# The first norm's root multiplies the products instead of the input

## The chip, the cores and the metric

One NeuronCore of a Trainium2 chip runs the kernel. The metric is device time in microseconds (us) of one execution.

## The reference

Two transformer blocks on x [256, 2048] in float32. What matters here is the first lines of the first block:

```
def _rmsnorm(x, w):
    y = x32 * lax.rsqrt(jnp.mean(x32 * x32, axis=-1, keepdims=True) + RMS_EPS)
    return (y * w.astype(jnp.float32)).astype(x.dtype)

u = _rmsnorm(h, norm_mix_w[l])                      # h = x, [256 tokens, 2048]
proj = jnp.einsum('btd,de->bte', u, w_in[l])        # w_in [2048, 11280]
(q_a, k_a, v_a, z_a, beta_a, dec_a, q_b, k_b, v_b, gate_a, gate_b) = jnp.split(proj, ...)
# q_a, k_a, v_a: causal convolution over 4 tokens, silu; then a gated delta rule with
# beta = sigmoid(beta_a), g = -exp(a_log) * softplus(dec_a + dt_bias)
# z_a: silu;  q_b, k_b, v_b: attention;  gate_a, gate_b: sigmoid
```

The root is one number for each token (row of x), so `proj = root * ((x * w) @ w_in)`: it can be multiplied before or after the product. The rest of the block (delta rule, attention, branch mix, feed-forward) and the second block stand behind this.

## The kernel before, in words

Every large product runs on TensorE in units. A unit is 256 rows of a weight matrix by 512 columns (512 KB). SyncE loads it into one of four slots of `raw` (RING = 4), ScalarE rounds it to `w_hi` (float32r), VectorE subtracts to get `w_lo`, and TensorE multiplies three times (hi by hi, lo by hi, hi by lo) against the input, which is split in the same way into `u_hi` and `u_lo`. The semaphores are `w_landed`, `hi_done`, `lo_done` and `w_used`; the load of a unit waits until the unit four before it has its `w_lo`, and the cast of a unit waits until TensorE has used the unit four before it. PLAN gives the order of the products: "qkv" (3 bodies of 16 units, 24 matmuls of 128x256 each unit, output transposed, channels on partitions), "spill" (8 bodies of 16 units, 12 matmuls of 128x512 each, tokens on partitions: z, q_b, k_b, v_b and the two gates), then "branch", "w_out", "ffn" and the products of the second block. A body makes 1024 columns, the first 512 in banks 0 and 1, the others in banks 2 and 3. Smaller work is put between the units by hand: each engine has callbacks (`first_due`, `between`) that run ahead of (ScalarE, VectorE) or behind (TensorE) unit j of a body.

The start. SyncE issues x in two halves of 128 tokens (1 MB each) with the constants `keep` (192 KB, the identity for transposes) between them, then the rows of `norm_mix_w`, four weight units, 17 small vectors, `ws_raw`, and the units from the fifth on. ScalarE squares each half of x with a sum (L1314), takes the root (L1306), casts the first unit. VectorE takes the reciprocal and multiplies x by it in pieces of 128x512 (`scaled_x`, L1939) into `xn`. TensorE transposes `xn`, four 128x128 tiles for each `turn_first(q)` (q = 0 to 7, two column blocks of x each, L709): q = 0 to 3 ahead of the first unit, q = 4, 5 behind unit 1 and q = 6, 7 behind unit 2. The transposes land in banks 4, 5, 2, 3 (FIRST_BANKS); ScalarE (`operand_high`, L1297) and VectorE (`operand_low`, L1917) multiply them by the norm weight's column and split them into `u_hi` and `u_lo`.

What uses the "qkv" and "spill" products. VectorE's `conv_pair` (L2003, L2005) reads a bank of the "qkv" product and does the four taps as 8 instructions of up to 256 elements on each partition; there are 12 such calls, q = 0 and 1 at j = 9 and 11 of a body, q = 2 and 3 at j = 1 and 3 of the next (the last two are in "spill"). `thin` makes the 16 logit columns (beta_a, dec_a) in bank 6 behind unit 10. `spill_drain` on ScalarE (L1384) reads a bank of the "spill" product with an activation and stores it. `delta_net` is a generator on each of the three engines that advances one step for each unit of "spill". Its first step on ScalarE (j = 0, ahead of the cast of that unit) is sigmoid of the beta logits (L1394) and exp of `a_log` (L1395); its first step on VectorE reads the other logits (L2045, L2047, L2051); ScalarE's next step (j = 1) is exp (L1400), ln (L1401) and the first square (L1418); TensorE's third step waits for ln and the square (L771). In the third "qkv" body and in "spill" VectorE also does a vector-matrix product for the modulation (`gemv`, L1874 to L1888), one 256 KB piece of weights for each unit, in two buffers; the load of a piece waits for the step on the piece before it (`gemv_step`).

Of the kernel before, what the change touches and what calls it, by code (L numbers as in the profile page):

```python
# [25 lines left out]
P = 128  # L26
T = 256
# [85 lines left out]
def block_kernel(nc, x, norm_mix_w, w_in, conv_w, a_log, dt_bias, gdn_o_norm_w, q_norm_w, k_norm_w,  # L113
# [5 lines left out]
    with ctx:  # L119
# [37 lines left out]
        xn = slot("xn", 7, [P, HALVES, D])  # L157
# [89 lines left out]
        def h_stage(q):  # L247
# [13 lines left out]
        E6, E5, QNS, BFC, MX, SUM, RCP, LAM, RELB, FCOL, CACT = (  # L261
            179, 180, 181, 182, 192, 256, 320, 384, 400, 416, 448)
# [83 lines left out]
        x_in = (sem("x_in0"), sem("x_in1"))  # L346
# [90 lines left out]


# [9 lines left out]
        def _(sp):  # L448
            loads = signal("vectors_in")
            for th in range(HALVES):  # L450
                sp.dma_start(xs[:, th], x[0][th * P:(th + 1) * P, :]).then_inc(x_in[th], 16)
                if th == 0:
                    sp.dma_start(keep[:], keep_const[:, 0:KEEP_W]).then_inc(signal("keep_in"), 16)
# [9 lines left out]
            dst, src = pairs[0]  # L463
            sp.dma_start(dst, src).then_inc(signal("mix_in"), 16)
            for j in range(RING):
                load(products["qkv"], 0, j, w_in[0], j, 0)
# [115 lines left out]
        def _(pe):  # L582
# [116 lines left out]
            pe.transpose(bank[SPARE][:, 3 * P:3 * P + KD], rows[0:KD, 0], ident[0:KD, 0:KD]).then_inc(signal("mix_sum"), 1)  # L699

            def turn_first(q):

                pe.wait_ge(signal("xn_ready"), HALVES * (q // 2 + 1))
# [3 lines left out]
                for f in range(2):  # L707
                    for th in range(HALVES):
                        ins = pe.transpose(b[:, f * T + th * P:f * T + (th + 1) * P],  # L709
                                           xn[:, th, (2 * q + f) * P:(2 * q + f + 1) * P], ident)  # L710
                ins.then_inc(turned, 1)

            for q in range(4):
                turn_first(q)
# [17 lines left out]
            def first_due(j):  # L732
                if j in (1, 2):
                    turn_first(2 * j + 2)
                    turn_first(2 * j + 3)
                if j == 4:
                    turn_rows()
                if j == 10:
# [505 lines left out]
        def _(act):  # L1244
# [64 lines left out]

            act.wait_ge(signal("constants_set"), 1)  # L1310
            own.link(act.activation(sm(RCP + 62), sm(E6), ACT.Sqrt, bias=sm(E6)))
            for th in range(HALVES):
                act.wait_ge(x_in[th], 16)
                own.inc(act.activation(xn[:, th], xs[:, th], ACT.Square, accum_out=sm(SS + th)))  # L1314
            own.wait()
            root(0, sm(SS, HALVES), sm(RR, HALVES), 1.0 / D, E6, "root_x")
# [58 lines left out]
            def spill_drain(pr, i, x):  # L1375
# [7 lines left out]
                for th in range(HALVES):  # L1383
                    act.activation(stage[:, x, th], acc[x][th][:], func).then_inc(drained[x], 1)  # L1384
# [7 lines left out]
            def delta_net():  # L1392
                act.wait_ge(signal("logits"), 1)
# [424 lines left out]
            for i in range(2):  # L1818
                def between(j, i=i):
# [3 lines left out]
                    if i == 0 and j == 10:  # L1823

                        act.wait_ge(signal("logits"), 2)
# [25 lines left out]
        def _(dve):  # L1851
# [84 lines left out]
            def scaled_x(c):  # L1936
                part = slice(c * COLS, (c + 1) * COLS)
                for th in range(HALVES):
                    dve.tensor_scalar(xn[:, th, part], xs[:, th, part], sm(RR + th), None, ALU.mult).then_inc(  # L1939
                        signal("xn_ready"), 1)  # L1940

# [7 lines left out]
            dve.wait_ge(signal("mix_sum"), 1)  # L1949
# [6 lines left out]
            first_low(0)  # L1956
            operand_low(0)
            first_low(1)
            operand_low(1)
            scaled_x(2)  # L1960
            operand_low(2)
            first_low(2)
            operand_low(3)
            first_low(3)
# [792 lines left out]
```

## Time and profile before

| | |
|---|---|
| median of 3 runs | 2657.59 us (2654.68 to 2659.8) |
| profiled execution | 2654.59 us, of which the span is 2652.8 us |
| TensorE matmul busy | 2586.1 us (97% of the span) |
| VectorE busy | 1796.1 us (68%) |
| ScalarE busy | 1171.8 us (44%) |
| DMA | 604.69 MB, mean 228 GB/s |

The span is from the first instruction to the last. TensorE's busy time counts pipelined matmuls and is no measure of its peak; idle time of an engine matters where TensorE waits for it. In timelines and groups, PE is TensorE, PEld its weight loads, DVE VectorE, ACT ScalarE, SPq the DMA queue of SyncE. Square brackets give the idle time ahead of an instruction and what ended it.

### The profile page before, as it was taken

What the parts mean: (1) busy time and instruction counts of PE and PEld (TensorE: products, weight loads), DVE (VectorE), ACT (ScalarE), POOL (GpSimd) and SP (SyncE); (2) the same over time, 40 slices, a digit from 0 to 9 for tenths busy, and PEclk for the clock granted to TensorE, in tenths of its full rate; (3) what the DMA queues carried; (4) which work ended last, traced back from release to release, by engine and by line L of the source; (5) the groups of instructions that cost most, each with busy time, mean ns of one, the idle gap of its engine ahead of it and who ended that gap; (6) DMA issues with size and microseconds to landing.
All of it is one profiled execution on the core that took longest, in us unless ns stands there. A gap on an engine that the chain in (4) does not pass through costs nothing.

```text
span 2652.8 us, 38762 instructions
## 1 busy us (share of the span) xinstructions
PE 2586.1 (97%) x14614; PEld 2175.5 (82%) x14614; DVE 1796.1 (68%) x2331; ACT 1171.8 (44%) x1475; POOL 0.2 (0%) x4
## 2 busy tenths in 40 slices
PE   8999999998999999999999999999999999999997
PEld 8977777777788778888887888899987778999885
DVE  6787676775567777777776666766786665545655
ACT  4454333454344544444443334333486344335642
POOL 0000000000000000000000000000000000000000
PEclk9999999999999999999999999999999999999998
DMA  7667676875768788888887777888845556665363
GB/s 209 195 234 249 218 229 208 276 254 192 250 209 269 260 270 269 275 274 271 272 275 246 251 249 254 278 273 272 252 141 182 181 167 183 182 215 165 123 224 125
DMA packets 313837, 604.69 MB, mean 228 GB/s; under 512 B 26670, under 2 KB 28724, under 8 KB 312028
## 3 DMA queue, kind: packets, MB, share of 16 engines
q1 hardware_dynamic: 301628, 571.59, 67.2%
q10 hardware_dynamic: 12064, 31.10, 3.2%
q8 instruction: 99, 1.62, 0.2%
q14 instruction: 46, 0.38, 0.0%
HBM read 591.98 MB, written 10.62 MB: 227 GB/s over the span
## 4 chain that ended last, share of the span: by engine, by line
PE 74%; DVE 2%; ACT 2%; issue 1%; DMA 1%; ACTq 0%; DVEq 0%; SPq 0%
PE bank L631 18%; PE bank L633 18%; PE bank L632 18%; PE bank L654 5%; PE bank L656 5%; PE bank L655 5%; PE bank L593 1%; PE bank L1091 1%; DVE w_lo L1858 1%; ACT w_hi L1254 0%; DMA raw<-in_w_branch_gdn 0%; PE bank L1102 0%; PE bank L1112 0%; PE bank L1088 0%; PE bank L1114 0%
## 5 line engine op out<-in xcount | busy, mean ns | idle before, releaser
L1858 DVE TENSOR_TENSOR w_lo<-raw,w_hi 128x1024 fp32r<-128x1024 f32 x820 | 1001.4, 1223 | 802.1 <-ACT w_hi L1254 801.0
L1254 ACT CAST w_hi<-raw 128x1024 fp32r<-128x1024 f32 x820 | 859.9, 1050 | 1371.7 <-PE bank L633 1028.2
L631 PE MATMUL bank<-w_hi,u_hi 128*128 128x512 f32 x1216 | 493.8, 406 | 3.1 <-DVE u_lo L1917 2.2
L632 PE MATMUL bank<-w_lo,u_hi 128*128 128x512 f32 x1216 | 483.8, 398 | 0.0
L633 PE MATMUL bank<-w_hi,u_lo 128*128 128x512 f32 x1216 | 483.2, 397 | 0.0
L1883 DVE SCALAR_TENSOR_TENSOR gemv_acc<-gemv_w,small,gemv_acc 128x512 f32<-128x512 f32 x480 | 357.8, 745 | 5.6 <-DMA gemv_w<-in_w_mod 5.2
L631 PE MATMUL bank<-w_hi,s_hi 128*128 128x512 f32 x768 | 311.1, 405 | 1.2 <-DVE w_lo L1858 1.1
L633 PE MATMUL bank<-w_hi,s_lo 128*128 128x512 f32 x768 | 304.6, 397 | 0.0
L632 PE MATMUL bank<-w_lo,s_hi 128*128 128x512 f32 x768 | 304.4, 396 | 0.0
L654 PE MATMUL bank<-s_hi,w_hi 128*128 128x256 f32 x1024 | 289.5, 283 | 0.0
L655 PE MATMUL bank<-s_lo,w_hi 128*128 128x256 f32 x1024 | 288.3, 282 | 0.0
L656 PE MATMUL bank<-s_hi,w_lo 128*128 128x256 f32 x1024 | 288.3, 282 | 0.0
L631 PEld LDWEIGHTS bank<-w_hi,u_hi 128*128 128x128 f32 x1216 | 230.3, 189 | 65.6 <-issue 8.1
L633 PEld LDWEIGHTS bank<-w_hi,u_lo 128*128 128x128 f32 x1216 | 230.3, 189 | 56.2
L632 PEld LDWEIGHTS bank<-w_lo,u_hi 128*128 128x128 f32 x1216 | 230.6, 190 | 51.5
L655 PEld LDWEIGHTS bank<-s_lo,w_hi 128*128 128x128 f32 x1024 | 193.2, 189 | 0.3
L656 PEld LDWEIGHTS bank<-s_hi,w_lo 128*128 128x128 f32 x1024 | 193.2, 189 | 0.0
L654 PEld LDWEIGHTS bank<-s_hi,w_hi 128*128 128x128 f32 x1024 | 192.0, 187 | 0.7 <-issue 0.3
L633 PEld LDWEIGHTS bank<-w_hi,s_lo 128*128 128x128 f32 x768 | 144.9, 189 | 35.3
L631 PEld LDWEIGHTS bank<-w_hi,s_hi 128*128 128x128 f32 x768 | 144.9, 189 | 34.8 <-DVE w_lo L1858 1.5
L632 PEld LDWEIGHTS bank<-w_lo,s_hi 128*128 128x128 f32 x768 | 145.2, 189 | 32.7
L631 PE MATMUL bank<-w_hi,hid_hi 128*128 128x512 f32 x352 | 140.0, 398 | 0.0
(356 smaller groups left out, 2903.5 us busy)
## 6 DMA issues: line engine op xcount, KB each, us to landing
gemv_w<-in_w_mod SPq DMA_DIRECT2D x384, 256.0 KB, 3.0
raw<-in_w_in SPq DMA_DIRECT2D x176, 512.0 KB, 4.5
raw<-in_a_w_in SPq DMA_DIRECT2D x128, 512.0 KB, 4.5
raw<-in_w_ffn_gate SPq DMA_DIRECT2D x88, 512.0 KB, 4.5
raw<-in_w_ffn_up SPq DMA_DIRECT2D x88, 512.0 KB, 4.1
raw<-in_w_ffn_down SPq DMA_DIRECT2D x88, 512.0 KB, 4.0
gemv_w<-in_kv_w_mod SPq DMA_DIRECT2D x128, 256.0 KB, 3.6
raw<-in_kv_w SPq DMA_DIRECT2D x64, 512.0 KB, 3.7
```

The source lines that it names most:

```text
L593: ins = pe.transpose(b[:, f * T + th * P:f * T + (th + 1) * P], src(f, th), ident)
L631: pe.matmul(o, xh, w_hi[:, s, t], start=(k == 0), stop=False)
L632: pe.matmul(o, xh, w_lo[:, s, t], start=False, stop=False)
L633: ins = pe.matmul(o, xl, w_hi[:, s, t], start=False, stop=(k == 2 * units - 1))
L654: pe.matmul(o, wh, hi[:, k], start=(k == 0 and f % 2 == 0), stop=False)
L655: pe.matmul(o, wh, lo[:, k], start=False, stop=False)
L656: ins = pe.matmul(o, wl, hi[:, k], start=False, stop=(k == 2 * half - 1 and f % 2 == 1))
L1091: ins = pe.matmul(b[:, P:3 * P], queries_of[p][:, a, P:T], k_t[:, a, 0:T], start=True, stop=not mask)
L1254: act.copy(w_hi[:, s], raw[:, s]).then_inc(hi_done, 1)
L1858: dve.tensor_tensor(w_lo[:, s], raw[:, s], w_hi[:, s].bitcast(F32), ALU.subtract).then_inc(lo_done, 1)
L1883: dve.scalar_tensor_tensor(out=gemv_acc[:], in0=w_k, scalar=c_k, in1=gemv_acc[:], op0=ALU.mult, op1=ALU.add).then_inc(gemv_step, 1)
```

## The change

x is loaded in three column parts (0:512, 512:1024, 1024:2048, each for all 256 tokens) instead of two token halves. The rows of `norm_mix_w`, weight units 0 and 1 and the third part of x are issued by ScalarE, the rest of the start by SyncE. TensorE transposes raw x (`xs`), so `xn` and `scaled_x` are gone: q = 0 and 1 ahead of the first unit, then two more behind each of units 0, 1 and 2. ScalarE squares x at j = 3 and 4 and takes the root at j = 5, VectorE the reciprocal at j = 6 (`RX`), TensorE spreads it over all partitions as a row at j = 7 (two matmuls of 128x128) and VectorE copies it to `rx_bc` at j = 8. The products are multiplied by it where they are read: `conv_pair` gets one 128x512 multiply ahead of its taps, `spill_drain` a per-partition scale, and the two groups of logits one multiply in place in bank 6, after which ScalarE's sigmoid may start.

```
 sync:
-            for th in range(HALVES):
-                sp.dma_start(xs[:, th], x[0][th * P:(th + 1) * P, :]).then_inc(x_in[th], 16)
-                if th == 0:
-                    sp.dma_start(keep[:], keep_const[:, 0:KEEP_W]).then_inc(signal("keep_in"), 16)
+            load_x(sp, 0)
+            sp.dma_start(keep[:], keep_const[:, 0:KEEP_W]).then_inc(signal("keep_in"), 16)
+            load_x(sp, 1)
+            load_first(sp, 2)
+            load_first(sp, 3)
...
-            dst, src = pairs[0]
-            sp.dma_start(dst, src).then_inc(signal("mix_in"), 16)
-            for j in range(RING):
-                load(products["qkv"], 0, j, w_in[0], j, 0)
 tensor:
             def turn_first(q):
-                pe.wait_ge(signal("xn_ready"), HALVES * (q // 2 + 1))
+                pe.wait_ge(x_in[min(q // 2, 2)], 16)
...
-            for q in range(4):
+            for q in range(2):
                 turn_first(q)
...
-                if j in (1, 2):
+                if j < 3:
                     turn_first(2 * j + 2)
                     turn_first(2 * j + 3)
...
+                if j == 7:
+                    pe.wait_ge(signal("rx_ready"), 1)
+                    for th in range(HALVES):
+                        ins = pe.matmul(bank[MODB][:, th * P:(th + 1) * P], sm(RX + th).broadcast_to([P, P]), ident,
+                                        start=True, stop=True)
+                    ins.then_inc(signal("first_sum"), 1)
 scalar:
+            dst, src = vector_rows()[0]
+            act.dma_start(dst, src).then_inc(signal("mix_in"), 16)
+            load_first(act, 0)
+            load_first(act, 1)
+            load_x(act, 2)
...
-            for th in range(HALVES):
-                act.wait_ge(x_in[th], 16)
-                own.inc(act.activation(xn[:, th], xs[:, th], ACT.Square, accum_out=sm(SS + th)))
-            own.wait()
-            root(0, sm(SS, HALVES), sm(RR, HALVES), 1.0 / D, E6, "root_x")
...
-            first_high(0)
             act.wait_ge(signal("cols_mix"), 1)
             for q in range(4):
                 operand_high(q)
-                if q < 3:
-                    first_high(q + 1)
+                first_high(q)
...
+                if j in (3, 4):
+                    own.inc(act.activation(x_sq[:, j - 3], xs[:, j - 3], ACT.Square, accum_out=sm(SS + j - 3)))
+                if j == 5:
+                    own.wait()
+                    root(0, sm(SS, HALVES), sm(RX, HALVES), 1.0 / D, E6, "root_x")
...
-                    act.activation(stage[:, x, th], acc[x][th][:], func).then_inc(drained[x], 1)
+                    act.activation(stage[:, x, th], acc[x][th][:], func, scale=sm(RX + th)).then_inc(drained[x], 1)
...
             def delta_net():
-                act.wait_ge(signal("logits"), 1)
+                act.wait_ge(signal("logits"), 2)
 vector:
-            dve.wait_ge(signal("root_x"), 1)
-            own.link(dve.reciprocal(sm(RR, HALVES), sm(RR, HALVES)))
-            scaled_x(0)
-            scaled_x(1)
...
+            for q in range(4):
+                operand_low(q)
+                first_low(q)
...
+                if j == 6:
+                    dve.wait_ge(signal("root_x"), 1)
+                    dve.reciprocal(sm(RX, HALVES), sm(RX, HALVES)).then_inc(signal("rx_ready"), 1)
+                if j == 8:
+                    dve.wait_ge(signal("first_sum"), 2)
+                    own.link(dve.tensor_copy(rx_bc[:], bank[MODB][:, 0:T]))
...
+                own.link(dve.tensor_tensor(over_x[:, q % 2], b[:].rearrange("p (f t) -> p f t", f=2), over_heads(rx_bc[:], 2), ALU.mult))
                 for tap in range(TAPS - 1, -1, -1):
...
-                        src = b[:, f * T:(f + 1) * T]
+                        src = over_x[:, q % 2, f]
...
                 dve.wait_ge(signal("logits"), 1)
+                dve.tensor_tensor(bank[SPARE][both, 0:T], bank[SPARE][both, 0:T], rx_bc[both], ALU.mult).then_inc(
+                    signal("logits"), 1)
+                dve.wait_ge(signal("logits"), 2)
```

The two helpers that it calls:

```
        X_PARTS = (slice(0, COLS), slice(COLS, 2 * COLS), slice(2 * COLS, D))
        def load_x(engine, n):
            part = X_PARTS[n]
            engine.dma_start(xs[:, :, part], halves(x[0])[:, :, part]).then_inc(x_in[n], 16)
        def load_first(engine, j):
            src = w_in[0][2 * P * j:2 * P * (j + 1), 0:COLS].rearrange("(t p) n -> p t n", p=P)
            engine.dma_start(raw[:, j], src).then_inc(w_landed[j], 16)
```

## Rows read from the trace of the kernel before

**Rows 1.** The page: busy time, share of the span and instructions of the engines.
```profile
PE 2586.1 (97%) x14614; PEld 2175.5 (82%) x14614; DVE 1796.1 (68%) x2331; ACT 1171.8 (44%) x1475; POOL 0.2 (0%) x4
```

**Rows 2.** Timeline of all engines, 0 to 40 us: start, length, engine, line, operation, tiles.
```profile
5.67 1.91 ACT L1314 ACTIVATE xn<-xs 128x2048 f32<-128x2048 f32 x1 [3.34 <-DMA xs<-in_x]
...
9.53 0.26 PE L699 MATMUL bank<-keep,rows 16*128 16x16 f32 x1 [9.53 <-DMA rows<-in_norm_mix_w]
...
12.69 3.67 PE L709 MATMUL bank<-keep,xn 128*128 128x128 f32 x16 [2.90 <-DVE xn L1939]
13.34 1.22 DVE L1944 TENSOR_TENSOR w_lo<-raw,w_hi 128x1024 fp32r<-128x1024 f32 x1
13.90 0.84 ACT L1297 ACTIVATE u_hi<-bank,cols 128x256 fp32r<-128x256 f32 x2 [1.45 <-PE bank L709]
...
14.63 1.04 ACT L1320 CAST w_hi<-raw 128x1024 fp32r<-128x1024 f32 x1
...
16.01 0.56 PE L654 MATMUL bank<-u_hi,w_hi 128*128 128x256 f32 x1
```

**Rows 3.** DMA from 0 to 30 us in 40 slices of 0.75 us.
```profile
GB/s 0 0 87 284 404 459 316 460 382 459 327 356 369 399 407 421 393 361 209 103 34 58 335 292 150 350 227 0 57 175 388 145 238 325 156 320 249 142 202 344
```

**Rows 4.** The tile `keep`, 0 to 20 us: its load (ns, start) and landing.
```profile
L453 SPq DMA_DIRECT2D keep<-in_keep_const x1: 420/420/420, 1.2 to 1.2; - x1
...
DMA to landing us min/median/max: 4.9/4.9/4.9
```

**Rows 5.** Timeline of TensorE and ScalarE in the first product.
```profile
16.80 0.41 PE L654 MATMUL bank<-u_hi,w_hi 128*128 128x256 f32 x1
17.01 0.37 PE L655 MATMUL bank<-u_lo,w_hi 128*128 128x256 f32 x1
...
22.37 1.04 PE L709 MATMUL bank<-keep,xn 128*128 128x128 f32 x8
...
30.12 1.05 ACT L1254 CAST w_hi<-raw 128x1024 fp32r<-128x1024 f32 x1 [0.85 <-PE bank L656]
33.00 1.05 ACT L1254 CAST w_hi<-raw 128x1024 fp32r<-128x1024 f32 x1 [1.83 <-PE bank L656]
```

**Rows 6.** Timelines of four engines around the start of the spill product.
```profile
162.19 0.34 SPq L484 DMA_DIRECT2D gemv_w<-in_w_mod  x1
...
165.05 0.75 DVE L1883 SCALAR_TENSOR_TENSOR gemv_acc<-gemv_w,small,gemv_acc 128x512 f32<-128x512 f32 x1 [1.75 <-DMA gemv_w<-in_w_mod]
...
165.26 0.38 ACT L1394 ACTIVATE gates<-bank 8x256 f32<-8x256 f32 x1
...
165.66 1.28 ACT L1395 ACT_TABLE_LOAD   x1
...
167.19 1.05 ACT L1254 CAST w_hi<-raw 128x1024 fp32r<-128x1024 f32 x1
...
169.16 0.48 DVE L2045 TENSOR_SCALAR gates<-bank,small 8x256 f32<-8x256 f32 x1
...
170.51 0.42 ACT L1400 ACTIVATE gates<-gates 8x256 f32<-8x256 f32 x1 [2.28 <-DVE gates L2051]
...
173.46 1.16 PE L771 MATMUL bank<-sq,pick 128*16 128x256 f32 x4 [2.21 <-ACT sq L1418]
```

**Rows 7.** Groups by line and form: count, busy us, mean ns of one, idle before.
```profile
L1384 ACT ACTIVATE stage<-bank 128x512 f32<-128x512 f32 x32 | 17.3, 594 | 0.1
...
L1482 ACT ACTIVATE qk_t<-bank,small 128x512 f32<-128x512 f32 x4 | 2.6, 686 | 2.4 <-PE bank L593 2.3
...
L2311 DVE TENSOR_TENSOR stage<-bank,gates 128x512 f32<-128x512 f32 x16 | 10.2, 681 | 0.0
```

**Rows 8.** Windows: busy of each engine, granted clock, DMA share, GB/s.
```profile
174.00:176.00 2.00, 2.00 (x7) 1.16 (x4) 1.97 (x5) 2.00 (x4) 0.00 (x0) 0.55 0.85 305
```

**Rows 9.** The chain that ended last, 600 to 612 us.
```profile
606.62 1.09 ACT stage L1384 x2
```

More of the change, by code:

```diff
@@ L156, in block_kernel @@
         u_lo = slot("u_lo", 5, [P, KD, T], F32R)
-        xn = slot("xn", 7, [P, HALVES, D])
+        x_sq = slot("x_sq", 7, [P, HALVES, D])
+        rx_bc = slot("rx_bc", 13, [P, T])
+        over_x = slot("over_x", 13, [P, 2, 2, T], extra=1024)
         ws_raw = slot("ws_raw", 9, [P, KD, 16])
@@ L260, in block_kernel @@
         LN_STATS, LN_MOMENTS = 336, 322
-        E6, E5, QNS, BFC, MX, SUM, RCP, LAM, RELB, FCOL, CACT = (
-            179, 180, 181, 182, 192, 256, 320, 384, 400, 416, 448)
+        E6, E5, QNS, BFC, RX, MX, SUM, RCP, LAM, RELB, FCOL, CACT = (
+            179, 180, 181, 182, 184, 192, 256, 320, 384, 400, 416, 448)
         c_act = small[:, CACT:CACT + KD]
@@ L345, in block_kernel @@
         turned, turn_hi, turn_free = sem("turned"), sem("turn_hi"), sem("turn_free")
-        x_in = (sem("x_in0"), sem("x_in1"))
+        x_in = (sem("x_in0"), sem("x_in1"), sem("x_in2"))
         gemv_landed = (sem("gemv_landed0"), sem("gemv_landed1"))
@@ L698, in _ @@
             pe.wait_ge(signal("mix_in"), 16)
-            pe.transpose(bank[SPARE][:, 3 * P:3 * P + KD], rows[0:KD, 0], ident[0:KD, 0:KD]).then_inc(signal("mix_sum"), 1)
+            pe.transpose(bank[SPARE][:, 3 * P:3 * P + KD], rows[0:KD, 0], ident[0:KD, 0:KD]).then_inc(signal("first_sum"), 1)
             def turn_first(q):
-                pe.wait_ge(signal("xn_ready"), HALVES * (q // 2 + 1))
+                pe.wait_ge(x_in[min(q // 2, 2)], 16)
                 if q >= 4:
@@ L709, in turn_first @@
                         ins = pe.transpose(b[:, f * T + th * P:f * T + (th + 1) * P],
-                                           xn[:, th, (2 * q + f) * P:(2 * q + f + 1) * P], ident)
+                                           xs[:, th, (2 * q + f) * P:(2 * q + f + 1) * P], ident)
                 ins.then_inc(turned, 1)
-            for q in range(4):
+            for q in range(2):
                 turn_first(q)
@@ L1823, in between @@
                     if i == 0 and j == 10:
-                        act.wait_ge(signal("logits"), 2)
+                        act.wait_ge(signal("logits"), 3)
                         ln_weights(0)
@@ L1934, in _ @@
             dve.memset(ws_lo[:].bitcast(F32), 0.0).then_inc(signal("ws_zero"), 1)
[L1936 to L1940, printed above, removed]
             def first_low(j):
@@ L1947, in operand_low @@
                 lo_of_turn(q, q % 4, u_lo[:, 2 * q:2 * q + 2], u_hi[:, 2 * q:2 * q + 2], MIX_W + 2 * q, FIRST_BANKS)
-            dve.wait_ge(signal("mix_sum"), 1)
+            dve.wait_ge(signal("first_sum"), 1)
             dve.tensor_copy(cols[:, 0:KD], bank[SPARE][:, 3 * P:3 * P + KD]).then_inc(signal("cols_mix"), 1)
-            dve.wait_ge(signal("root_x"), 1)
-            own.link(dve.reciprocal(sm(RR, HALVES), sm(RR, HALVES)))
-            scaled_x(0)
-            scaled_x(1)
             dve.wait_ge(signal("cols_mix"), 1)
[L1956 to L1964, printed above, removed]
-            scaled_x(3)
+            for q in range(4):
+                operand_low(q)
+                first_low(q)
             def first_due(j):
@@ L2043, in delta_net @@
                 logits = bank[SPARE][hd, 0:T]
+                both = slice(0, 32 + H1)
                 dve.wait_ge(signal("logits"), 1)
+                dve.tensor_tensor(bank[SPARE][both, 0:T], bank[SPARE][both, 0:T], rx_bc[both], ALU.mult).then_inc(
+                    signal("logits"), 1)
+                dve.wait_ge(signal("logits"), 2)
                 dve.tensor_scalar(gates8[hd, 0], logits, sm(DTB, 1, 32, 40), 0.0, ALU.add, ALU.min).then_inc(
@@ L2705, in _ @@
                 body("v3", i, value_drain, between)
-            dve.wait_ge(signal("logits"), 2)
+            dve.wait_ge(signal("logits"), 3)
             z = bank[SPARE][0:H3, 0:T]
```

## The prediction

> **What bounds the kernel now.** The page comes first. TensorE is busy for 97% of the span [rows 1], so whatever starts TensorE earlier, or makes it wait, moves the end by as much, and work on other engines costs nothing unless TensorE comes to wait for it. The change touches four places only: the start, the convolutions, the logits and the drains of "spill". For each I read the timeline of the engines and ask what TensorE waits for there.
>
> At the start TensorE does nothing before 9.53, turns x from 12.69 on and begins the first unit at 16.01 [rows 2]. From there it has no gap: ScalarE's casts, each released by the end of a unit, stand 2.88 us apart (30.12 to 33.00), which is the price of a unit, 0.12 us for each of its 24 matmuls [rows 5]. The last matmuls before 17.2 start 0.21 us apart (16.80, 17.01) [rows 5], the pace of the 1.2 GHz level; the later ones run at 2.4 GHz. From 16.01 to 30.12, where unit 3 ends, there are four units (11.5), two groups of 8 transposes of 1.04 each (2.1) and about 0.6 for the slow first matmuls: 14.2 against 14.1 read.
>
> The next gap of TensorE in the stretch that the change touches is at 171: it idles 2.2 us until 173.46, put down to ScalarE's square [rows 6]. Behind the square stands a serial chain: VectorE's gates (169.16) release ScalarE's exp (170.51), then a table load, ln and the square. It is on the path, and it is where the change adds work.
>
> **The start.** Removed from the path: the squares (1.91 each, the first started when x had landed at 5.67), root, reciprocal and scaling. What then sets the first unit is the identity in `keep`, which every transpose needs. It is issued at 1.2 and lands 4.9 us later, at 6.1 [rows 4]; until then 1.25 MB (half of x, then it) had been asked for on its queue. With slices of 0.75 us the DMA row gives 1.16 MB moved by 5.25 and 1.5 MB by 6.0 [rows 3], so landing comes some 0.6 us behind the bytes. After the change 0.52 MB of x and 0.2 MB of `keep` stand on SyncE's queue, and ScalarE's queue moves about as much in the meantime: 1.45 MB, at about 5.9, landed at 6.6. The Trainium skill, "DMA: Bandwidth & Descriptors", section "Issuing engines are not separate DMA queues", says that transfers issued by several engines interleave on the same DMA engines and that this only saves issue time; no row of before has two busy queues at the start, so nothing here tests it, and by it the split buys no bandwidth. By bounds from rows: not before 6.1, where it lands today behind more bytes of its own queue; the other end is the third rival below.
>
> From 6.6: the small transpose and the first four of x. From the first transpose of x to ScalarE's first `u_hi` is 1.2 us today (12.69 to 13.90), with 0.15 more for the small one: 7.95. Two `u_hi` pieces until the cast starts take 0.73 (13.90 to 14.63), the cast 1.04, `w_lo` 1.22 [rows 2]: 7.95 + 0.73 + 1.04 + 1.22 = 10.95, say 11.0 for the first unit. That is 5.0 earlier than 16.01.
>
> Given back: one more group of 8 transposes now stands behind the first unit, 1.04; two broadcast matmuls behind unit 7, at the transposes' 0.13 each, 0.3 with their loads. And the lower level: today it costs unit 0 about 0.6, behind 16 transposes without a pause. After the change only 8 come first and TensorE idles about 2 us before unit 0. If all 24 matmuls of unit 0 then start 0.21 apart instead of 0.12, that costs 2.2, 1.6 more than today; at the other end it costs what it does now, 0 more. I take 1.1, nearer the upper end, since the run-up is half as long and followed by an idle stretch. Gain 5.0 - 1.04 - 0.3 - 1.1 = 2.6 us; bounds: 5.5 - 1.34 = 4.2 and, with `keep` 1 us later, 4.0 - 1.34 - 1.6 = 1.1.
>
> Does anything else become late? ScalarE's `u_hi` for q = 2 waits for transposes that now come behind unit 0, about 16: with cast and `w_lo` unit 2 is ready at 19.0, and TensorE wants it at about 20.4. So it is covered, by 1.4 us. The squares at j = 3 and 4 put 2.1 us each in front of two casts; a cast is needed three units (8.6 us) later and ScalarE idles 1.8 us of each 2.88: at nothing. SyncE issues three transfers fewer before the small vectors, and the next weight load then waits for `lo_done`, as before. The reciprocal and copy on VectorE stand ahead of casts that have the same ring of slack: at nothing.
>
> **The convolutions.** Each of 12 calls gets a multiply of 128x512 from a bank, 0.68 (the group at L2311) [rows 7], and a wait for its own result, some 0.06. In bodies 1 and 2 VectorE is idle part of each unit, and a late `w_lo` has the ring before it. What remains is the third body, where gemv leaves VectorE without idle time: its last idle before 169 ends at 165.05 with a landed gemv piece [rows 6], whose load was issued at 162.19, right when VectorE had finished the step before. So that idle time does not absorb a delay; it moves with it. Two calls at j = 9 and 11: 1.5 us at most, 0 at least if the backlog clears before; I take 1.0, since the load waits on VectorE's step.
>
> **The logits.** Today the wait chain is 169.16 to 173.46, 4.30 us [rows 6]. ScalarE had done sigmoid, a table load, exp and a cast long before (165.26 to 168.2), under cover of VectorE's backlog. The change makes sigmoid wait for VectorE's multiply, which comes at 169.16 plus the delay above. So on the path now: the multiply, 0.48 (as L2045, a read of the same bank); sigmoid, the exp table and exp, 167.19 - 165.26 = 1.93; the cast, 1.05; then exp to TensorE's resumption, 173.46 - 170.51 = 2.95, and 0.04 for the semaphore. That is 6.45, plus 1.0 of delay: 7.45 against 4.30, a gap longer by 3.15 us (2.15 to 3.65). Queued behind the waiting sigmoid are the cast of unit 4 of "spill", exp, ln and the square; behind the cast is VectorE's `w_lo`. TensorE needs that unit two units after it resumes, so only the square is waited for.
>
> The table load behind sigmoid takes 1.28 and the next activation starts with it done [rows 6]. The Trainium skill, "ScalarE: Activation LUTs", section "What ACT_TABLE_LOAD costs", puts a switch at about 2.66 us with a drain behind the load; the row shows no drain. By the page the one load newly on the path would cost 1.4 us more and the sum would be 1.4 us longer.
>
> The clock: after today's gap of 2.2 us the granted clock reads 0.55 from 174 to 176 [rows 8]. A gap of 5.4 us is followed by at least as long a slow stretch; between nothing and 0.7 us more, I take 0.3.
>
> **The drains.** 32 activations of 128x512 get a scale from memory: without one 594 ns (L1384), with one 686 (L1482) [rows 7]. Most lie under the matmuls. Four pairs, all like the one at 606.62, are links of the chain that ended last [rows 9], 0.18 each: 0.7 us (0 to 0.9).
>
> **The sum.** Start -2.6, gap +3.15, clock +0.3, drains +0.7: +1.5 us. On the profiled execution, 2652.8 of span and 1.8 around it, that is 2654.6 + 1.5 = 2656.1. The median of the runs shown is 3.0 above this execution, so the time is 2657.6 + 1.5 = 2659.1. By the bounds: -4.2 + 2.15 = 2.0 less, 2655.6, and -1.1 + 3.65 + 0.7 + 0.9 = 4.15 more, 2661.8.
>
> **The rivals.** (1) The gap at 171 does not grow: VectorE's multiply is ready when ScalarE comes, as the unit work has slack there. Then 2.6 is gained, 0.7 lost: 2655.7. Against it stands that VectorE has no idle time from 165.05 to 169.16. (2) Each table switch costs more than its row once it is on the path, 1.4: 2660.5; against it, the activation at 167 follows its load at once. (3) Slower: the two queues do not share evenly, and `keep` arrives behind the 2.1 MB of ScalarE's queue. Then 3.35 MB must move first, 10.8 in the DMA row, landed at about 11.4: unit 0 starts at 15.9, the start loses 2.4 (1.04 + 0.3 + 1.1) instead of gaining 2.6, and the time is 2664.1. It decides against the change (over 5.3 us) from a landing of about 10.3 on. For it: `keep` itself landed only 0.6 us behind its bytes today, so any bytes put ahead of it count in full; against: it would take a strict preference for one queue, of which no row speaks. (4) Faster: the start gains all of 4.2 and the gap at 171 disappears because the taps, which now read a tile instead of a bank, shorten VectorE's backlog. The gap gives 2.2, its slow clock 0.9 (0.45 of the 2 us of that window), the drains take 0.7: 6.6 less, 2651.0. It decides from 5.3 us on. Against it: ScalarE's sigmoid and cast, 3 us, stand on the path whenever VectorE is done.
>
> **How the numbers follow.** A measurement of this kernel tells about 0.2%, 5.3 us, from no change. Forecast 0.52, rival 1 0.14, rival 2 0.09: all within it. Rival 3 0.09 and other waits of that size 0.08: slower 0.17. Rival 4 and the like with over 5.3 us: faster 0.08. So 0.08, 0.75, 0.17. The range reaches from 2653.5, the lower bound of the sum, 2655.6, and part of the way to rival 4, up to rival 3 at 2664; it leaves out about 1 in 10 on either side.
>
> **What would show it.** Right: the first unit near 11; unit 3 ends near 27.4; TensorE's gap near 168 is about 5.4 us long, still released by the square; sigmoid follows VectorE's multiply; drains of 686 ns. Wrong: `keep` landing after 8; a wait for `w_lo` in units 1 to 3; the gap unchanged; new gaps behind the convolutions in the third body.

## The result and the profile after

| | before | after |
|---|---|---|
| median of 20 runs each | 2655.83 us (2652.25 to 2661.05) | 2660.89 us (2657.14 to 2662.56) |
| ratio of the times, over all runs | | 1.0018, 95% interval 1.0011 to 1.0024 |
| profiled execution | 2654.59 us | 2662.56 us, span 2660.8 |

The kernel became slower by 5.06 us. (The ratio is worked out from all the runs, so its last digit can differ from that of the two medians.) The whole interval lies above 1, and its middle just inside the 0.2%, or 5.3 us, that the prediction calls no change. The profiled execution of after is the slowest of its 20 and the one of before lies 1.2 us under its median, so these two traces are 8.0 us apart; the sections below say which part of that is the change.

The busy row of the page, beside [rows 1]:

```profile
PE 2591.3 (97%) x14618; PEld 2179.0 (82%) x14618; DVE 1800.3 (68%) x2337; ACT 1174.1 (44%) x1475; POOL 0.2 (0%) x4
```

It tells little: VectorE has 4 us more work, ScalarE 2 us. The timeline tells the rest. First the start of after, against [rows 2, 5]:

```profile
6.21 0.28 PE L710 MATMUL bank<-keep,rows 16*128 16x16 f32 x1 [6.21 <-DMA keep<-in_keep_const]
6.42 1.97 PE L720 MATMUL bank<-keep,xs 128*128 128x128 f32 x8
...
7.66 0.84 ACT L1314 ACTIVATE u_hi<-bank,cols 128x256 fp32r<-128x256 f32 x2 [3.15 <-PE bank L720]
8.39 1.04 ACT L1337 CAST w_hi<-raw 128x1024 fp32r<-128x1024 f32 x1
...
9.46 1.23 DVE L1958 TENSOR_TENSOR w_lo<-raw,w_hi 128x1024 fp32r<-128x1024 f32 x1
...
10.83 0.55 PE L665 MATMUL bank<-u_hi,w_hi 128*128 128x256 f32 x1 [2.45 <-DVE w_lo L1958]
...
14.60 0.39 PE L667 MATMUL bank<-u_hi,w_lo 128*128 128x256 f32 x1
14.81 0.29 PE L665 MATMUL bank<-u_hi,w_hi 128*128 128x256 f32 x1
```

The identity ends TensorE's first wait, at 6.1 as before, and the first unit starts at 10.83, 5.2 earlier. But TensorE idles 2.45 us ahead of it, and its matmuls stay 0.21 us apart until 14.81 (18 of the 24; before it was 5). At the end of the third unit of "spill" after is 2.50 us ahead (TensorE's gap starts at 168.74, before at 171.24): that is what the start is worth in this pair of executions. In the traces of the same start in experiments 1, 2, 3, 4 and 7 the gap starts between 168.25 and 170.03, with this one 168.8 on average, and in a second trace of the kernel before (experiment 11) at 170.93: by the means 2.3 us.

Then the gap behind which the squares stand, against [rows 6]:

```profile
168.52 0.42 DVE L2056 TENSOR_TENSOR bank<-bank,rx_bc 40x256 f32<-40x256 f32 x1
...
169.02 1.28 ACT L1414 ACT_TABLE_LOAD   x1 [5.89 <-DVE bank L2056]
...
170.31 0.37 ACT L1414 ACTIVATE gates<-bank 8x256 f32<-8x256 f32 x1
170.70 1.28 ACT L1415 ACT_TABLE_LOAD   x1
172.00 0.20 ACT L1415 ACTIVATE small<-small 8x1 f32<-8x1 f32 x1
172.23 1.04 ACT L1271 CAST w_hi<-raw 128x1024 fp32r<-128x1024 f32 x1
173.30 0.41 ACT L1420 ACTIVATE gates<-gates 8x256 f32<-8x256 f32 x1
...
173.73 1.28 ACT L1421 ACT_TABLE_LOAD   x1
...
175.03 0.42 ACT L1421 ACTIVATE gates<-gates 8x256 f32<-8x256 f32 x1
...
175.47 0.63 ACT L1438 ACTIVATE sq<-conv_out 128x512 f32<-128x512 f32 x1
...
176.24 1.87 PE L788 MATMUL bank<-sq,pick 128*16 128x256 f32 x4 [7.50 <-ACT sq L1438]
```

The gap is 7.50 us instead of 2.21. ScalarE has been idle for 5.89 us when VectorE's multiply releases it, and then does three table loads on TensorE's path instead of one. Before, the first of them stood far ahead of the gap:

```profile
163.97 1.28 ACT L1394 ACT_TABLE_LOAD   x1
```

TensorE's clock behind the gap, by windows of 2 us (the eighth figure, behind the five engines' busy times, is the granted clock), against [rows 8]:

```profile
170.00:172.00 2.00, 0.00 (x0) 0.00 (x0) 0.30 (x1) 1.96 (x4) 0.00 (x0) 0.96 0.73 271
172.00:174.00 2.00, 0.00 (x0) 0.00 (x0) 0.69 (x1) 1.93 (x4) 0.00 (x0) 0.50 0.00 1
...
180.00:182.00 2.00, 2.00 (x6) 1.56 (x5) 1.90 (x5) 0.07 (x1) 0.00 (x0) 0.50 0.09 14
182.00:184.00 2.00, 2.00 (x10) 0.95 (x9) 1.94 (x3) 0.98 (x1) 0.00 (x0) 0.98 0.94 296
```

The lower level holds from 172 to 182, and from 176.24 TensorE works at it; before it held from 174.2 to 177.6. Each window between the two pairs shown reads 0.50 too. The distance of the two traces grows from 2.78 us at the end of the gap (173.46 and 176.24) to 3.90 at 251.39 and 255.29, where TensorE waits next.

These 1.1 us can't be put down to the longer gap. From the end of the gap to the next wait it is 77.93 us before and 79.05 after, but 79.23 in the second trace of the kernel before, whose gap is 2.71. The other traces with such a gap lie between 77.73 (experiment 3, with the longest gap, 7.68) and 79.19 (experiment 1, with 3.72). How long the lower clock outlasts the gap differs between executions of one program by as much as this term.

The groups by line and form that answer to [rows 7], and last the one of before that takes the place of L2013:

```profile
L1404 ACT ACTIVATE stage<-bank,small 128x512 f32<-128x512 f32 x32 | 20.2, 683 | 0.1
...
L2015 DVE SCALAR_TENSOR_TENSOR conv_out<-over_x,cols,conv_out 128x255 f32<-128x255 f32 x24 | 10.6, 481 | 0.4
...
L2005 DVE TENSOR_TENSOR over_x<-bank,rx_bc 128x512 f32<-128x512 f32 x12 | 8.2, 684 | 0.0
L2013 DVE TENSOR_SCALAR conv_out<-over_x,cols 128x256 f32<-128x256 f32 x24 | 7.4, 351 | 0.4
...
L2003 DVE TENSOR_SCALAR conv_out<-bank,cols 128x256 f32<-128x256 f32 x24 | 10.4, 476 | 0.0
```

Both new prices, 683 and 684 ns, came as predicted. Where the slower drains reach TensorE shows in its later gaps. Two of them, before, then after:

```profile
576.08 0.49 PE L835 MATMUL bank<-qk_t 128*128 128x128 f32 x2 [0.21 <-ACT qk_t L1482]
...
610.40 0.49 PE L835 MATMUL bank<-qk_t 128*128 128x128 f32 x2 [3.10 <-ACT probs L1501]
```

```profile
580.54 0.49 PE L852 MATMUL bank<-qk_t 128*128 128x128 f32 x2 [0.39 <-ACT qk_t L1502]
...
615.08 0.49 PE L852 MATMUL bank<-qk_t 128*128 128x128 f32 x2 [3.30 <-ACT probs L1521]
```

With a third (3.47 to 3.69, at 648 and 653) these gaps grow by 0.18, 0.20 and 0.22, and they have these two lengths, to 0.03, in every trace without and with the scale. Two more gaps grow in this pair, 0.98 to 1.21 at 551 and 3.96 to 4.30 at 704, but they differ by as much between traces of the same kernel (the second of before has 1.14 and 2.84). The distance is 5.30 at 703.70 and 709.00, 1.4 more than at 251. The sum for this pair: 2.5 gained, 5.3 in the gap, 1.1 for the clock behind it, 1.4 from there to 709: 5.3 us slower, where the medians say 5.06. How near the two figures come is in part luck, since the last two terms differ from trace to trace.

All the traces together give a firmer price of the drains. From the wait at 251 to the one at 704 the six traces without the scale (before, and experiments 3, 4, 6, 10, 11) take 451.2 to 452.7 us, on average 452.0; the seven with it (after, and 1, 2, 5, 7, 8, 9) take 452.6 to 455.4, on average 453.8. That is 1.9 us, though the two ranges touch; the three of the six that have the new start (3, 4, 10) take 451.7 on average.

What comes later is 2.7 us more, 8.0 at the end: a stretch of the lower clock behind 707 is 6.8 us long instead of 3.4, and there is one at 892 in after (0.51 and 0.64 in the windows from 892 to 896) and none in before. The code there is the same. Experiment 11 is about this, and it leaves it open.

### The profile page after: what moved, and what is told of

It reads as the page before. It is cut to its first block, busy times and chain, and to the rows that moved or that the text cites. A ratio compares the mean times of both kernels' runs of the same rounds, so it can differ in the third digit from the quotient of the medians.

```text
span 2660.8 us, 38777 instructions
## 1 busy us (share of the span) xinstructions
PE 2591.3 (97%) x14618; PEld 2179.0 (82%) x14618; DVE 1800.3 (68%) x2337; ACT 1174.1 (44%) x1475; POOL 0.2 (0%) x4
## 4 chain that ended last, share of the span: by engine, by line
PE 90%; DVE 4%; ACT 3%; DMA 2%; issue 2%; ACTq 0%; DVEq 0%; SPq 0%
PE bank L642 21%; PE bank L644 21%; PE bank L643 21%; PE bank L665 6%; PE bank L667 6%; PE bank L666 6%; PE bank L604 1%; PE bank L773 1%; DMA gemv_w<-in_w_mod 1%; ACT w_hi L1271 1%; DVE w_lo L1878 1%; DVE gemv_acc L1903 1%; PE bank L1108 1%; DMA raw<-in_w_branch_gdn 0%; DVE conv_out L2015 0%
```

## The experiments

The time differences are between medians, each against runs of the kernel before on the same chip: 2656.94 (33 runs) for 1 to 4, 2657.48 (33 runs) for 5 to 8, 2657.71 (13 runs) for 9 and 10. The kernels of 1 to 8 ran 11 times each, 9 eight times, 10 six times, 11 and 12 once. The ratios are worked out from the single runs, not from the medians; where the two differ, as in 1, 4 and 6, the difference is within the interval. All but 6, 11 and 12 are edits of the changed kernel. "Gap" is TensorE's gap that the square ends.

| | time | difference | ratio, interval | gap |
|---|---|---|---|---|
| 1 logits early | 2657.42 | +0.5 | 0.9999 [0.9990, 1.0008] | 3.72 |
| 2 convolutions plain | 2659.57 | +2.6 | 1.0009 [1.0000, 1.0019] | 4.84 |
| 3 drains plain | 2660.60 | +3.7 | 1.0012 [1.0003, 1.0021] | 7.68 |
| 4 start only | 2653.10 | -3.8 | 0.9990 [0.9981, 0.9999] | 1.96 |
| 5 gates early | 2652.22 | -5.3 | 0.9981 [0.9972, 0.9990] | none |
| 6 before, gates early | 2651.68 | -5.8 | 0.9981 [0.9972, 0.9990] | none |
| 7 table first | 2659.09 | +1.6 | 1.0008 [0.9999, 1.0017] | 5.93 |
| 8 start filled | 2661.39 | +3.9 | 1.0013 [1.0004, 1.0022] | 6.84 |
| 9 = 5 and 8 | 2650.30 | -7.4 | 0.9973 [0.9962, 0.9983] | none |
| 10 = 5 and 3 | 2650.53 | -7.2 | 0.9972 [0.9959, 0.9984] | none |

**1. The logits are multiplied in the second "qkv" body**, not in `delta_net`. (`...` stands for what is cut from a line.)

```
 vector, qkv body between(j):
+                    if i == 1 and j == 5:
+                        dve.wait_ge(signal("logits"), 1)
+                        dve.tensor_tensor(bank[SPARE][both, 0:T], bank[SPARE][both, 0:T], rx_bc[both], ALU.mult).then_inc(signal("logits"), 1)
 vector, delta_net():
-                dve.wait_ge(signal("logits"), 1)
-                dve.tensor_tensor(bank[SPARE][both, 0:T], ... , rx_bc[both], ALU.mult).then_inc(signal("logits"), 1)
```

> The changed kernel with VectorE's multiply of the logits moved from the first step of the delta rule (in the spill product) to unit 5 of the second qkv body, where VectorE has idle time; all else as changed. Theory A (the gap of TensorE before the first squares grew from 2.2 to 7.5 us, 3.4 of it because sigmoid, with the load of its table, waits for this multiply, and 1.9 because VectorE's backlog in the third body grew by four multiplies of 0.48 net): the gap falls to 2.2 + 1.9 = 4.1 us, the sigmoid runs before it under cover, and the time is 3.4 to 4 us under the changed kernel, about +1.3 us against the kernel before. Rival B (VectorE's backlog alone decides when the chain behind the gap starts, and the sigmoid's wait is hidden): the gap stays at 7 us and the time at about +5.

ScalarE's timeline in this kernel:

```profile
162.82 1.28 ACT L1414 ACT_TABLE_LOAD   x1
164.11 0.37 ACT L1414 ACTIVATE gates<-bank 8x256 f32<-8x256 f32 x1
164.50 1.28 ACT L1415 ACT_TABLE_LOAD   x1
...
169.21 0.42 ACT L1420 ACTIVATE gates<-gates 8x256 f32<-8x256 f32 x1 [2.12 <-DVE gates L2067]
```

Sigmoid and both loads are back under VectorE's backlog and the gap falls from 7.50 to 3.72. So the wait on the multiplied logits makes up 3.8 us of the gap, and 4.6 us of the 5.06 by the medians. The two intervals don't overlap. From VectorE's first read of the logits to TensorE's resumption it is 4.30 again, as before; what is left of the gap above 2.21 is that VectorE comes 1.50 us later against TensorE.

**2. The convolutions read the bank again**, without the root.

```
-                own.link(dve.tensor_tensor(over_x[:, q % 2], b[:]..., over_heads(rx_bc[:], 2), ALU.mult))
-                        src = over_x[:, q % 2, f]
+                        src = b[:, f * T:(f + 1) * T]
```

> The changed kernel without the 12 multiplies by the root ahead of the convolution taps: the taps read the bank as before, so q, k and v of the delta rule miss the root (this part is left out of the computation). Theory A: VectorE reaches the logits 1.9 us earlier against TensorE, the gap is 5.6 instead of 7.5 us, the time 1.9 to 2.3 us under the changed kernel, about +3 us against before. Rival B2 (the gap comes from the wait of the sigmoid alone; the idle time of VectorE ahead of 164 and 166, which ended with a landed piece of weights, takes up the multiplies): gap 7.5, time +5.

```profile
165.38 0.42 DVE L2055 TENSOR_TENSOR bank<-bank,rx_bc 40x256 f32<-40x256 f32 x1
...
173.09 1.86 PE L788 MATMUL bank<-sq,pick 128*16 128x256 f32 x4 [4.84 <-ACT sq L1438]
```

From VectorE's multiply to TensorE's resumption it is 7.71 here and 7.72 in after: the serial chain has its own length, and the convolutions only set when it starts. By VectorE's first read of the logits it starts 2.87 us ahead of the gap here, 2.34 in experiment 4, and 2.08 and 1.59 in the two traces of the kernel before; with the multiplies in the convolutions it starts only 0.22 (after), 0.04 (3), 0.51 (7), 0.58 (1) and 0.88 us (8) ahead. By the means, 2.2 and 0.4, the convolutions hold VectorE up by 1.8 us.

**3. The drains have no scale**; q_b, k_b, v_b, z and the gates lack the root.

```
-                    act.activation(stage[:, x, th], acc[x][th][:], func, scale=sm(RX + th)).then_inc(drained[x], 1)
+                    act.activation(stage[:, x, th], acc[x][th][:], func).then_inc(drained[x], 1)
```

> The changed kernel with the drains of the spill product without the root as scale (left out: z, q_b, k_b, v_b and the two gates miss the root). Theory A: 32 activations of 594 instead of 686 ns, of which four pairs to seven pairs lie on TensorE's path: 0.7 to 1.4 us under the changed kernel, about +4 us against before. Rival B3 (the drains are covered by the matmuls and the later growth of the distance is noise of one execution): no change, +5.

The gaps that end at 614.61 and 651.88 are 3.09 and 3.46 again, as before, and 1.4 us of the time is gone (+3.7 instead of +5.06, of two chips, with intervals that overlap, so the medians alone don't show it). In its trace all 24 matmuls of unit 0 are 0.21 apart, against 18 in after. This number varies between executions: with this start and no filling it is 13 to 24 in eight traces, and the unit takes 4.3 to 5.3 us.

**4. The new start alone**: 2 and 3 together, and no multiply of the logits.

> The changed start alone: parts of x, raw transposes, and the root worked out and spread over the partitions as in the change, but no product is multiplied by it (the root is left out of the whole first norm). Theory A: first unit at 10.8, unit 3 ends 2.5 to 2.9 us earlier than before, the gap is 2.2 us again, and the time is 2.5 us under the kernel before (-2.5, down to -3). Rival B4 (the earlier start is given back at the next wait for loads, or by a longer stretch at the lower clock, whatever is done to the products): 0 against before.

The time falls by 3.8 us by the medians and by 2.7 by the ratio (0.3 to 5.0 by the interval), with the gap at 1.96 instead of 2.21, where 2.5 was expected for the start. It is the only part of the change that gains.

**5. All the gates early**: the multiply and VectorE's three instructions on the logits at unit 5 of the second body, ScalarE's sigmoid and exp at unit 7, exp and ln at unit 8. **6** does the same in the kernel before.

```
 vector, between(j):                        scalar, between(j):
+  if i == 1 and j == 5: first_gates()     +  if i == 1 and j == 7: sigmoid, exp(a_log)
                                           +  if i == 1 and j == 8: exp, ln
```

> The changed kernel with the whole first part of the gates moved from the first two steps of the delta rule into the second qkv body, where VectorE and ScalarE have idle time: the multiply of the logits and VectorE's three gate instructions at unit 5, ScalarE's sigmoid and exp at unit 7, its exp and ln at unit 8. All of the computation is kept. Theory A (the gap of TensorE before the first squares is the serial chain of logits, sigmoid, exp, ln and square): the gap is gone, with the stretch at the lower clock behind it, and against the kernel before the time is -2.5 (start) - 2.2 - 1.1 (gap and its slow clock) + 0.7 to 1.4 (drains) = about -4.7 us. Rival C (TensorE then waits for the next thing that VectorE's backlog makes late, w_lo of the first spill units): a gap of 3 us or more stays and the time is -1 to +1 against before.

> The kernel before the change, with only the same move of the gates into the second qkv body. Theory A: its gap of 2.2 us and the lower clock behind it (1.1 us) go: about -3.3 us against the kernel before. Rival C: another wait takes the place of the gap, 0 to -1 us. The distance between this kernel and the changed one with early gates is what the earlier start is worth when no chain behind it grows: by theory A 2.5 - 0.7 to 1.4 = 1.1 to 1.8 us in favour of the changed one.

TensorE in experiment 5, timeline and one window:

```profile
169.33 0.39 PE L644 MATMUL bank<-w_hi,u_lo 128*128 128x512 f32 x1
169.65 1.04 PE L788 MATMUL bank<-sq,pick 128*16 128x256 f32 x4
...
170.61 0.50 PE L642 MATMUL bank<-w_hi,u_hi 128*128 128x512 f32 x1
```

```profile
174.00:176.00 2.00, 2.00 (x10) 0.97 (x8) 1.97 (x4) 1.52 (x3) 0.00 (x0) 1.00 0.44 170
```

There is no gap and no lower clock behind it, and both kernels beat the kernel before by 5 to 6 us. So the gap was never a price of the products: all of it, the old 2.2 us too, is three short gate steps waiting in the wrong place. The kernel before gained 5.8 us by this (2.7 to 7.4 by the interval) where 3.3 was expected, the changed one 5.3 for 4.7. But the second expectation failed. I expected 1.1 to 1.8 us in favour of the new start, and the medians differ by 0.5 the other way, with equal ratios. The traces say why in part: experiment 5 is 2.06 us ahead at 246.04 (248.10), 0.65 at 606.59 and 0.35 at 700.48, so most of the start's gain is lost where the drains are. From there to the end it loses 2.7 us more (1951.8 against 1949.1), in code that is the same; experiment 11 comes back to this.

**7. The sigmoid's table is loaded ahead of the wait**, by an activation of one column.

```
 scalar, delta_net():
+                own.link(act.activation(sm(RCP + 62), sm(E6), ACT.Sigmoid))
                 act.wait_ge(signal("logits"), 2)
```

> The changed kernel with one added instruction on ScalarE, a sigmoid of one column, ahead of its wait for the multiplied logits, so that the load of the sigmoid table (1.28 us) runs before the wait ends. Theory A: the gap falls from 7.5 to 6.2 us and the time by 1.3 us, up to 1.8 with the clock, to about +3.6 us against before. Rival D (a table load ends with something more than its 1.28 us row, a drain of 1.4 us by the notes on the chip): the fall is up to 2.7 us, to +2.4. Rival E (the table load was hidden before the wait anyway): +5.

```profile
162.99 1.28 ACT L1413 ACT_TABLE_LOAD   x1
164.28 0.20 ACT L1413 ACTIVATE small<-small 128x1 f32<-128x1 f32 x1
168.57 0.37 ACT L1415 ACTIVATE gates<-bank 8x256 f32<-8x256 f32 x1 [4.09 <-DVE bank L2057]
168.96 1.28 ACT L1416 ACT_TABLE_LOAD   x1
170.26 0.20 ACT L1416 ACTIVATE small<-small 8x1 f32<-8x1 f32 x1
```

The load goes under cover and the gap shrinks by 1.57, to 5.93: 1.28 is the load, and in this trace VectorE comes 0.29 earlier against TensorE than in after. By the times alone (+1.6 and +5.06, with intervals that overlap) this would not be shown; it is by the rows. The activation behind a load starts 0.01 to 0.02 us after it, on the path as off it: a load costs its 1.28 and nothing behind it.

**8. TensorE is kept busy ahead of unit 0** by 11 transposes of the identity into an unused bank.

```
             for q in range(2):
                 turn_first(q)
+            for _ in range(11):
+                pe.transpose(bank[MODB][:, 0:P], ident, ident)
```

> The changed kernel with 11 transposes of the identity into an unused bank between the first 8 transposes of x and the first unit, in the 2.45 us in which TensorE idles there. Theory A: the first unit still starts at 10.8, but its matmuls come to the pace of the 2.4 GHz level earlier; in the changed kernel 18 of 24 start 0.21 us apart, 1.6 us lost, against 0.6 us before the change. So 1.0 to 1.6 us less, about +3.8 us against before. Rival F (what the idle stretch holds makes no difference to when the clock rises): no change, +5; if the filling ran over, +5.5.

The mechanism works (5 matmuls of unit 0 at the slow pitch, where the eight traces without the filling have 13 to 24). The time is where it was expected, +3.9 for +3.8, but that can't be told from after's +5.06, and at the gap nothing is gained: it starts at 168.77, in after at 168.74. The reason is in its trace: TensorE waits 1.27 us, until 157.20, for a `w_lo` that VectorE starts at 155.93, when a convolution with its new multiply (from 151.95) lets go of it. So the convolutions cost TensorE here before the logits do, and what the filling gains is lost at this place. (The prediction had named a new gap in this body as a sign of being wrong; after has none there, experiments 3, 7 and 10 have 0.30, 0.18 and 0.30.)

**9. 5 and 8 together.**

> The changed kernel with the gates moved into the second qkv body and the idle stretch before the first unit filled with 11 transposes of the identity: the two changes that made it faster or nearly so, together; all of the computation is kept. Theory A: the start is worth its full 5.2 us of earlier first unit less 1.3 us of transposes and broadcast, 3.7 instead of 2.5, so about 1.2 us less than with the gates early alone, -6.5 us against the kernel before (-5.3 was measured for the gates alone). Rival G (what the fill gives is smaller than what one stretch more at the lower clock takes later): no different from the gates alone, -5.3.

The start of this kernel:

```profile
8.23 2.55 PE L728 MATMUL bank<-keep 128*128 128x128 f32 x11
10.89 0.55 PE L666 MATMUL bank<-u_hi,w_hi 128*128 128x256 f32 x1
11.24 0.33 PE L667 MATMUL bank<-u_lo,w_hi 128*128 128x256 f32 x1
```

Unit 0 runs almost at once at 0.12 us a matmul, and at the row of 246.04 in experiment 5 this kernel stands at 243.60, 2.4 us ahead. It computes all that the reference does, and at 7.4 us under the kernel before it is the fastest complete version by the medians; its interval overlaps those of 5 and 6.

**10. 5 without the scale in the drains**; as in 3, z, q_b, k_b, v_b and the gates lack the root.

> The changed kernel with the gates moved into the second qkv body and the drains of the spill product without the root as scale (left out: z, q_b, k_b, v_b and the two gates miss the root). With the gates early the changed start was worth nothing against the old start (0.9981 for both), where theory A had 1.1 to 1.8 us. Theory H (the rest of the 2.5 us goes to the drains, whose ScalarE work lies on TensorE's path in 5 to 7 places, 1.4 us to 1.7 us in all): -5.3 - 1.5 = about -6.8 us against before, and TensorE stays over 1.5 us ahead of the old start's trace at 700 us. Rival I (it goes to the clock, which falls behind the gap at 882 us in the changed kernels): no change, -5.3.

At the rows where experiment 5 stands at 246.04, 606.59 and 700.48 this one stands at 245.46, 604.32 and 697.38: the distance grows from 0.58 to 2.27 and 3.10. The first 0.58 is the slow pitch of unit 0 (5.26 us in 5, 4.70 in 10), the rest 1.7 us by 607 and 2.5 by 700; by the medians the two kernels are 1.9 apart, of two chips. The larger part of the 1.7 is not on the chain that the prediction read: TensorE waits for `w_lo` at 536 (0.55) and 547 (1.00) in 5, once (0.56) in 10. This pair lies a little above the 1.9 us that all the traces give.

**11. The kernel before again**, for the 2.7 us behind 709.

> The kernel before, once more, for one more profile: 7 of 8 changed kernels' profiles show one stretch more at the lower clock behind the gap of TensorE at 882 us (1.7 us lost), and neither of the two profiles with the old start does. If the clock there depends on the chance of the execution (theory J), this profile shows it with a chance of one half or so; if on something that the change does (rival K), it does not show it.

Its windows behind the gap that ends at 885.4:

```profile
886.00:888.00 2.00, 2.00 (x7) 1.60 (x6) 2.00 (x3) 0.00 (x0) 0.00 (x0) 0.60 0.73 269
888.00:890.00 2.00, 2.00 (x6) 1.53 (x6) 0.93 (x2) 0.00 (x0) 0.00 (x0) 0.55 0.87 241
```

In the first profile of the same kernel both windows from 884 to 888 read 1.00. So the kernel before can show the stretch too, and whether a gap of some 2 us is followed by the lower level differs from one execution to the next. But this does not clear the change. The stretch shows in all ten traces of changed kernels and in one of the three with the old start. From the wait at 704 to the end those ten take 1950.7 to 1951.9 us, on average 1951.6, and the three 1949.1 (before), 1949.1 (6) and 1950.8 (this one). Why is open. This execution's gap at 171 was 2.71 and its stretch behind it 6.8 long, instead of 2.21 and 3.4.

**12. Experiment 6 again**, for one more trace with the old start.

> The kernel before with the gates in the second qkv body, once more, for one more profile of the old start. Theory J (chance of the execution): the stretch at the lower clock behind the gap at 882 us shows in this profile or in the other; rival K (the change's doing): in neither, and the part from 700 us to the end is 1949 us long again, against 1951.8 us in the changed kernels.

This gave nothing on the question. The one execution took 9692.43 us; the same kernel's 11 runs have a median of 2651.68. Its timeline on TensorE:

```profile
1000.91 1.62 PE L633 MATMUL bank<-w_hi,u_lo 128*128 128x512 f32 x1
1002.18 1.79 PE L631 MATMUL bank<-w_hi,u_hi 128*128 128x512 f32 x1
```

Matmuls that start 0.23 us apart in experiment 6 start 1.3 us apart here, while the granted clock reads 1.0 and VectorE's and ScalarE's busy times are as ever. I can't explain it, and draw nothing from it.

## Why the prediction was partly right

Forecast was +1.5 us (2659.1), measured +5.06 (2660.89). The time lies inside the range and in the likeliest case, no change of over 5.3 us, but only by 0.2 us. The difference was too small by 3.6 us; the time itself is off by only 1.8, because the 20 runs of the kernel before have a median 1.8 us under that of the 3 runs that the forecast was built on. That part is luck. The reasons for the 3.6 us:

- **The start: right.** 2.6 predicted, 2.5 read (2.3 by the means of all traces); unit 0 at 10.83 for 11.0. `keep` landed 4.9 us after its issue as before, which refutes rival 3. Experiment 4 gives 3.8 by the medians and 2.7 by the ratio, with 2.5 in its interval. The slow pitch of unit 0, taken at 1.1 us more than before, cost 1.2 in this pair (4.71 us for the unit, 3.48 before).
- **The logits: the step that failed.** "ScalarE had done sigmoid, a table load, exp and a cast long before" was read rightly, but the sum of the new path, 1.93 from sigmoid on, leaves out the load ahead of sigmoid, which in the trace of before stands at 163.97, just above the rows I took. It is issued behind the wait and so waits too: 1.28 us. Experiment 7 takes it out and shows it.
- **The convolutions: half their number.** The prediction counted two calls in the third body, 1.0. There are four (q = 2 and 3 of the body before come at j = 1 and 3), and each is dearer by 3.99 - 3.51 = 0.48: the multiply 0.68 and its wait 0.04, less 0.25 because the two TENSOR_SCALAR of a call take 351 ns from the tile and 476 from the bank. 4 x 0.48 = 1.92; VectorE reached the logits 1.86 us later than the start's gain would have put it, and the traces with and without the multiplies give 1.8. That the idle time ahead of gemv moves with the work, as the prediction had it, is borne out: 1.38 and 0.67 us in after, 1.75 before.
- **With both, the gap:** 3.15 + 1.28 + 0.86 = 5.29, read 5.29 (7.50 - 2.21). Rivals 1 and 4 (it does not grow, or goes) fall with it, and rival 2 with the rows of experiment 7. It fell outside my bound of 3.65.
- **The clock: 1.1 in this pair for 0.3, but not shown to be the change's.** The lower level outlasted the gap by 5.8 us of work, for 4.1 before (173.46 to 177.6), but 6.2 in the second trace of the kernel before and 3.0 in experiment 3 with its gap of 7.68. That a longer gap is followed by "at least as long a slow stretch" does not hold, and "0.7 at most" had no row behind it.
- **The drains: some 1.9 instead of 0.7.** The price of 683 ns was right, the places were too few: the prediction took four links of the chain that ended last. Three gaps of TensorE grow by 0.2 each in every trace with the scale; the rest of the 1.9 us is spread over waits whose length varies. This pair has 1.4 and experiment 10 has 2.5, all over the bound of 0.9.

Open: why the part behind 704, where the code is the same, took on average 1.9 us more in the traces of changed kernels than in the three with the old start. Either the change makes the stretch of lower clock there likelier, or three traces are too few. The forecast has no term for it, and so the 5.06 us can't be divided among the terms to better than 1 to 2 us. The gap, with 5 us, is well clear of that.

## What to carry to other kernels

Moving a factor from the input of a product to its output takes it off one path and puts it in front of every reader. Ask of each reader not what the multiply costs but which serial chain starts there; here the wait for 0.4 us of multiply made one gap 3.8 us longer. A wait in front of an activation holds its table load as well: read the rows above the one that waits. And when a small chain of another engine decides a gap, look first whether it can run earlier. Moving the gates forward 70 us was worth 5.8 us on the kernel before alone (2.7 to 7.4), and the new start, without the products' multiplies, 3.8 (0.3 to 5.0). And before a difference of 1 us between two traces is explained, look how far two traces of the same kernel lie apart.

## What the runs showed of the hardware that I had not expected

- A table load belongs to its activation: behind a wait it starts only when the wait ends (169.02, 5.89 us idle), and sigmoid, exp and ln need three loads of 1.28 us in a row.
- TENSOR_SCALAR of 128x256 takes 351 ns from a tile in SBUF and 476 from a bank; SCALAR_TENSOR_TENSOR of about the same size takes 480 from either.
- After a start with 8 transposes and 2.45 us idle, 13 to 24 of the first 24 matmuls ran at the 1.2 GHz pitch (eight traces); with 11 more transposes in the idle time 5 and 1 did (two traces), and before, with 16 transposes without a pause, 5, 4 and 1 (three).
- The same program shows the lower clock behind a gap of some 2 us in one execution and not in the next (experiment 11). Two traces of the kernel before differ by 1.3 us from the gap at 171 to the next wait and by 1.7 from 704 to the end: more than most terms of the sum.
